# Gathering the rows of two expert pairs in one pass, and the place of the seventh pair's gate weights in the load order

## The chip, the core and the metric

The kernel runs on one core of one Trainium2 chip. The metric is the device time of one launch in microseconds (us). The whole model, a mixture-of-experts block followed by two further layers, is a single program; each engine (TensorE as PE, VectorE as DVE, ScalarE as ACT, GpSimd as POOL) runs its own instruction list and waits on semaphores, and SyncE (SP) issues the weight loads.

## The reference, cut to what matters

The change lies in the mixture of experts of the first block. 256 tokens of width 1024, 16 experts with a hidden width of 512, two experts for each token:

```
def hierarchical_moe(h, w_rg, b_rg, w_re, b_re, w_gate, w_up, w_down):
    ...
    gates = (onehot_g[:, :, None] * w_group[:, None, :]).reshape(-1, N_EXPERTS).astype(t.dtype)
    out = jnp.zeros_like(t)
    for e in range(N_EXPERTS):
        hid = jax.nn.silu(t @ w_gate[e]) * (t @ w_up[e])
        out = out + gates[:, e:e + 1] * (hid @ w_down[e])
    return out.reshape(b, s, d)
```

All of it is float32. What follows, `second_block`, reads `out` after a layer norm and is not touched.

## The kernel before, in words

An expert handles up to 64 tokens ("slots") in a round, and two experts, a **pair**, share the 128 columns of a tile. There are eight pairs, numbered here 0 to 7 (so "pair 6" is the seventh). With these inputs one round is enough, so each pair runs once. Pairs come in twos: an even and an odd one form the body of a loop (`even_and_odd`), whose last turn, pairs 6 and 7, stands behind the loop.

For a pair TensorE does, in this order (`expert_pair`):

- the **gate** product into bank M0 and the **up** product into M1: each is 16 float32 matmuls of 512 columns, two experts side by side, and shows as 32 rows of L1142
- the **scatter** of the pair before, L1106: 8 matmuls that add its output rows to their tokens in S and PT
- four transposes of the hidden rows, L1151, and the turned pick matrix and gate column, L1156 and L1158
- the **gather** of the next pair's rows, L1096: a product of `h_rows` (the tokens) with `pick` (a 0/1 matrix of 256 tokens by 128 slots), in float32, 16 rows into bank MO and 16 into MX
- the **down** product into MO and MX, L1171, which needs the hidden tile that VectorE copies (L2916)

ScalarE copies the gathered rows out of MO and MX (L2031) into `taken_t`; VectorE makes the pick matrices (L2856). Ahead of the loop one gather serves pair 0.

The six weight chunks of a pair (gate, up and down for each expert, 2 MB each) are loaded by SyncE in an order written by hand (`load_gates`, `load_up`, `load_rest`), one queue, strictly one after the other. Gate weights and the first up chunk have two places each, one for even and one for odd pairs. The second up chunk (`up1`) and both down chunks have one place, so they can only be asked for when the pair before has used them up. The waits say so: `gate_done(q)` is M0 filled by pair q, `up_done(q)` is M1 filled, and a down chunk waits for MX to be filled by the pair before.

```
            for p in range(1, PAIRS):
                if p < 4:
                    load_next(p + 1)
                load_rest(p, p, PAIR_CHUNKS[3:4])
                if p == 4:
                    load_next(p + 1)
                load_rest(p, p, PAIR_CHUNKS[4:])
                if 4 < p < PAIRS - 1:
                    load_next(p + 1)
```

Here `load_next(p)` loads the gates and the first up chunk of pair p, `PAIR_CHUNKS[3:4]` is `up1` and `PAIR_CHUNKS[4:]` the two down chunks. For p = 5 the queue is thus: up1 of pair 5, down of pair 5, gates of pair 6, first up chunk of pair 6.

Of the kernel before, what the change touches and what calls it, by code (L numbers as in the profile page):

```python
# [29 lines left out]
F32 = mybir.dt.float32  # L30
# [259 lines left out]
def two_blocks(nc, t, out):  # L290

    with ExitStack() as ctx, nc.allow_non_contiguous_dma(reason="small vectors turned onto partitions"):
# [44 lines left out]
        rounds_f = sb("rounds_f", [P, 5])  # L337
        rounds_i = sb("rounds_i", [1, 4], I32)
# [53 lines left out]
        pick = view(at, TB, P)  # L392
        pick_g = view(at + SEQ, TB, P)
        gate_pair, gate_slot = view(at + 5 * D + 320, TB, 2), view(at + 5 * D + 324, 1, 1)
        taken_t = view(at + D, KD, P)
# [4 lines left out]
        gate_of = view(at + 4 * D + 768, TB, PICKS)  # L400
# [104 lines left out]
        pair_high, pair_low = h_t_r[:, 0:KF, :].rearrange("p k n -> p (k n)"), h_t_r[:, KF:KD, :].rearrange("p k n -> p (k n)")  # L505
# [103 lines left out]
        pick_ready, pick_g_ready = sem("pick_ready"), sem("pick_g_ready")  # L609
        expert_tanhed = sem("expert_tanhed")  # L610
# [41 lines left out]
        def out_count(b, q, last):  # L652

            return b.nth("moe", "taken" if last else "out", q)
# [5 lines left out]
        def _(pe):  # L660
# [427 lines left out]
            def gather(q, name="taken"):  # L1088

                pe.wait_ge(pick_ready, q + 1)  # L1090
                for j, b in enumerate((MO, MX)):
                    claim(b, name, q - 1)
                    for i in range(4):
                        k = 4 * j + i
                        for tb in range(TB):
                            ins = pe.matmul(b.ap[:, i * P:(i + 1) * P], h_rows[:, tb, k * P:(k + 1) * P], pick[:, tb, :],  # L1096
                                            start=tb == 0, stop=tb == TB - 1)
                    ins.then_inc(b.full, 1)

# [14 lines left out]
            gather(0, "taken")  # L1114
# [6 lines left out]
            for b in (MO, MX):  # L1121
                pe.wait_ge(b.free, b.nth("start", "taken"))
            last_even = pe.value_load(rounds_i[0:1, 3:4], min_val=PAIRS - 2, max_val=PAIRS * ROUNDS - 2)
            def expert_pair(q, gate_landed, gate_w, up_landed, up_w, last=False):
# [8 lines left out]
                for b in (MO, MX):  # L1133
                    pe.wait_ge(b.free, q * 2 + 1)
# [3 lines left out]
                for kind, b in enumerate((M0, M1)):  # L1138
                    both_w = [weights_of(e, kind) for e in range(2)]
                    for k in range(KD):  # L1140
                        for lanes, w in zip(halves, both_w):
                            ins = pe.matmul(b.ap[lanes, :], taken_t[:, k, lanes], w[k], start=k == 0, stop=k == KD - 1)  # L1142
                    ins.then_inc(b.full, 1)
                for y in (MO, MX):
                    pe.wait_ge(y.free, q * 2 + 2)
# [14 lines left out]
                if not last:  # L1160
                    gather(q + 1)
# [4 lines left out]
                for half, y in enumerate((MO, MX)):  # L1166
                    if not last:
                        claim(y, "out", q)
# [9 lines left out]
            def even_and_odd(q, last=False):  # L1178
                expert_pair(q, [(expert_landed[e], q * 8 + 16) for e in range(2)], even_w,
# [2192 lines left out]
```

## Time and profile before

| | |
|---|---|
| median of three runs | 1680.19 us (1678.5 to 1682.64) |
| the profiled execution | 1683.05 us |
| its span, first to last instruction | 1681.3 us |
| mean granted TensorE clock | 0.986 |
| PE busy | 1595.3 us, 95% |
| DVE busy | 939.9 us, 56% |
| ACT busy | 653.9 us, 39% |
| the expert pairs | from 359.2 us to 582 us of the span |
| load queue from 340 to 600 us | 91.6% of the 16 DMA engines' time |

Columns of a timeline row: start and length in us, engine, line, operation, output<-inputs, tile shape, count, and in brackets how long the engine sat idle before it and what ended that. A busy PE is one with a matmul in flight; two column halves run side by side, so L1142 at 0.59 us each starts one couple every 0.43 us. The rows of SPq are the issues of loads, not the transfers; the time from issue to landing is a separate line.

### The profile page before, as it was taken

Reading aid. Unit: us, or ns where it says so; the run is one execution under the profiler, and the core shown is the slowest. Engines: PE = TensorE matmul, PEld = TensorE weight load, DVE = VectorE, ACT = ScalarE, POOL = GpSimd, SP = SyncE. Lnnn points to the kernel's source line nnn. Section 1 sums busy time; section 2 is a strip of 40 time slices with the busy share of each in tenths; the row PEclk is TensorE's granted clock in tenths of the full one; section 3 lists DMA queues with packets and bytes.
Section 4 is the critical chain, followed back from the end, with each engine's and each line's share of the span. In section 5 each row is a group of like instructions: output and inputs, shape, how many; then the busy total and the mean of one; then the engine's idle time right before and its main releaser. Section 6 shows DMA issues by size and latency. Waiting matters only on the chain.

```text
span 1681.3 us, 22363 instructions
## 1 busy us (share of the span) xinstructions
PE 1595.3 (95%) x9359; PEld 1239.7 (74%) x9359; DVE 939.9 (56%) x1374; ACT 653.9 (39%) x960; POOL 27.1 (2%) x89
## 2 busy tenths in 40 slices
PE   5999999999999889899999999999999999999998
PEld 1998655454445378687888899988768878889986
DVE  3876666642222265565685666545466567556653
ACT  2543410111111243565644543435365744543441
POOL 1000010100000000000000000000000000000000
PEclk9999999989999989999999999999999999999999
DMA  8555518889989924423354455545424235435651
GB/s 306 189 186 200 202 51 292 328 360 412 413 356 423 390 99 149 126 96 109 145 177 153 143 172 188 200 150 193 153 76 151 101 126 182 169 122 192 201 178 73
DMA packets 153090, 333.33 MB, mean 198 GB/s; under 512 B 17699, under 2 KB 69157, under 8 KB 140709
## 3 DMA queue, kind: packets, MB, share of 16 engines
q1 hardware_dynamic: 147440, 326.94, 53.7%
q10 hardware_dynamic: 5558, 5.06, 0.9%
q8 instruction: 70, 1.15, 0.3%
q14 instruction: 22, 0.18, 0.0%
HBM read 330.94 MB, written 1.05 MB: 197 GB/s over the span
## 4 chain that ended last, share of the span: by engine, by line
PE 80%; DVE 8%; DMA 6%; ACT 4%; issue 1%; POOL 0%; ACTq 0%; POOLq 0%; DVEq 0%; SPq 0%
PE ps_g L737 19%; PE ps_g L718 16%; PE ps_g L1142 6%; PE ps_g L1282 6%; PE ps_s L1538 4%; PE ps_p L1538 3%; PE ps_o L785 3%; PE ps_g L878 3%; DMA arena<-in_w_up_dram 3%; PE ps_p L718 2%; DVE ring_r L2292 2%; DMA ring<-in_w_mod_dram 2%; PE ps_s L718 1%; PE ps_x L691 1%; PE ps_o L1171 1%
## 5 line engine op out<-in xcount | busy, mean ns | idle before, releaser
L2292 DVE TENSOR_TENSOR ring_r<-ring,late_w 128x4096 fp32r<-128x4096 f32 (+1 forms) x50 | 216.9, 4339 | 153.6 <-ACT late_w L1854 153.6
L1854 ACT ACTIVATE late_w<-ring 128x4096 fp32r<-128x4096 f32 (+1 forms) x50 | 178.1, 3563 | 127.9 <-PE ps_p L1538 42.8
L737 PE MATMUL ps_g<-hf_high,ring_r 128*128 128x256 f32 x640 | 178.8, 279 | 0.0
L737 PE MATMUL ps_g<-hf_high,late_w 128*128 128x256 f32 x576 | 162.1, 281 | 0.0
L737 PE MATMUL ps_g<-h_t_r,late_w 128*128 128x256 f32 x576 | 161.2, 280 | 0.0
L737 PEld LDWEIGHTS ps_g<-hf_high,ring_r 128*128 128x128 f32 x640 | 121.9, 190 | 0.0
L737 PEld LDWEIGHTS ps_g<-h_t_r,late_w 128*128 128x128 f32 x576 | 108.6, 189 | 0.0
L737 PEld LDWEIGHTS ps_g<-hf_high,late_w 128*128 128x128 f32 x576 | 108.1, 188 | 0.0
L1878 ACT ACTIVATE arena<-arena,neg_max 128x256 f32<-128x256 f32 (+1 forms) x160 | 71.5, 450 | 40.7 <-DVE neg_max L2347 40.7
L1142 PE MATMUL ps_g<-arena 128*64 128x512 f32 x288 | 85.9, 599 | 0.0
L718 PE MATMUL ps_g<-early_w,first_low 128*128 128x512 f32 (+1 forms) x176 | 68.7, 391 | 3.7 <-ACT arena L1840 1.8
L785 PEld LDWEIGHTS ps_o<-arena 128*128 128x128 f32 x496 | 61.3, 191 | 13.2 <-issue 9.1
L1282 PE MATMUL ps_g<-gate_w,first_low 128*128 128x512 f32 x160 | 67.4, 421 | 1.6 <-ACT arena L2148 1.6
L718 PE MATMUL ps_g<-early_w,h_t_r 128*128 128x512 f32 (+1 forms) x176 | 68.6, 390 | 0.0
L2292 DVE TENSOR_TENSOR ring_r<-ring,early_w 128x4096 fp32r<-128x4096 f32 (+2 forms) x12 | 47.6, 3968 | 36.9 <-ACT early_w L1854 36.9
L718 PE MATMUL ps_g<-ring_r,first_low 128*128 128x512 f32 (+1 forms) x176 | 68.2, 387 | 0.0
L785 PE MATMUL ps_o<-arena 128*128 128x64 f32 (+1 forms) x496 | 61.4, 273 | 6.3 <-ACT arena L1893 3.1
L1282 PE MATMUL ps_g<-gate_w,h_t_r 128*128 128x512 f32 x160 | 63.0, 394 | 0.0
L1282 PE MATMUL ps_g<-ring_r,first_low 128*128 128x512 f32 x160 | 62.9, 393 | 0.0
L2292 DVE TENSOR_TENSOR ring_r<-ring,first_w 128x4096 fp32r<-128x4096 f32 x11 | 48.7, 4425 | 24.7 <-ACT first_w L1854 24.7
L3052 DVE TENSOR_TENSOR ring_r<-ring,gate_w 128x1024 fp32r<-128x1024 f32 x40 | 48.4, 1219 | 24.3 <-ACT gate_w L2123 23.9
L1142 PE MATMUL ps_g<-ring,arena 128*64 128x512 f32 x192 | 55.6, 592 | 2.2 <-issue 2.2
(697 smaller groups left out, 3713.6 us busy)
## 6 DMA issues: line engine op xcount, KB each, us to landing
ring<-in_w_in_dram SPq DMA_DIRECT2D x31, 2048.0 KB, 7.8
ring<-in_w_gate_up_dram SPq DMA_DIRECT2D x44, 1024.0 KB, 7.2
arena<-in_w_down_dram SPq DMA_DIRECT2D x16, 2048.0 KB, 13.5
ring<-in_w_mod_dram SPq DMA_DIRECT2D x10, 2048.0 KB, 10.3
ring<-in_w_down_dram SPq DMA_DIRECT2D x10, 2048.0 KB, 8.0
arena<-in_w_up_dram SPq DMA_DIRECT2D x8, 2048.0 KB, 17.7
ring<-in_w_gate_dram SPq DMA_DIRECT2D x8, 2048.0 KB, 14.5
ring<-in_w_up_dram SPq DMA_DIRECT2D x4, 2048.0 KB, 18.3
```

Source lines behind the costliest of these rows:

```text
L691: ins = pe.transpose(b.ap[0:size, i * SEQ + tb * P:i * SEQ + (tb + 1) * P], piece(tb), ident[:, :])
L718: ins = pe.matmul(b.ap[:, 0:n], x[:, k, tb * P:(tb + 1) * P], a[:, k, lo:lo + n], start=k == 0 and i == 0, stop=k == nk - 1 and i == len(b ...
L737: ins = pe.matmul(b.ap[:, (f % 2) * SEQ:(f % 2 + 1) * SEQ], a[:, k, f * P:(f + 1) * P], x[:, k, :], start=k == 0 and i == 0, stop=k == nk ...
L785: ins = pe.matmul(O.ap[:, i * width:(i + 1) * width], probs_t[:, i, b, :], v(step, i, b), start=b == 0, stop=b == kbs - 1)
L878: ins = pe.matmul(b.ap[:, :], x[:, k, tb * P:(tb + 1) * P], w[:, k, :], start=k == 0, stop=k == KD - 1)
L1142: ins = pe.matmul(b.ap[lanes, :], taken_t[:, k, lanes], w[k], start=k == 0, stop=k == KD - 1)
L1282: ins = pe.matmul(G[tb].ap[:, :], x[:, 2 * q + k, tb * P:(tb + 1) * P], a[:, k, :], start=q == 0 and k == 0 and i == 0, stop=q == KD // 2 ...
L1538: ins = pe.matmul((S, PT)[tb].ap[:, half * HALF:(half + 1) * HALF], a[:, k, tb * P:(tb + 1) * P], x[:, k - 4 * c, half * HALF:(half + 1) * ...
L1854: act.activation(high_of(name, rnd)[:, 0:n], ring[:, slot, 0:n], ACT.Copy).then_inc(high_ready.sem, 1)
L1878: ins = act.activation(s, s, ACT.Exp, bias=neg_max[:, n % 2, i:i + 1], scale=-1.0, accum_out=den[:, n % 4, i:i + 1])
L2292: dve.tensor_tensor(ring_r[:, slot, 0:n], ring[:, slot, 0:n], high_of(name, rnd)[:, 0:n].bitcast(F32), ALU.subtract).then_inc(low_ready.se ...
L3052: dve.tensor_tensor(gate_piece(name, q, ring_r), gate_piece(name, q, ring), gate_high_w[q].bitcast(F32), ALU.subtract).then_inc(gate_low, 1)
```

## The change

Three things are done.

1. The rows of two pairs are gathered at once. `pick` becomes `pick_r`, 256 slots wide. Ahead of the loop there are now two float32 gathers (`first_gather`, pairs 0 and 1). In the loop the gather stands in the odd pair only (`gather_two`) and fetches both pairs of the next turn. It is no longer one float32 product but two in the faster `float32r` format: `h_rows` is split into a high part, made by ScalarE (`routed_high`, four copies), and a low part, made by VectorE (`routed_low`, four subtractions). `taken_t` holds 256 slots, and its second half lies in `h_t`; `pair_low` moves to the arena.
2. Four fillings of MO and MX belong to such a gather in place of two, so the semaphore counts of the down chunks change (`out_count`).
3. For p = 5 the gates of pair 6 are asked for ahead of the down chunks of pair 5, and the first up chunk behind them.

```diff
-            def gather(q, name="taken"):
-
-                pe.wait_ge(pick_ready, q + 1)
+            def first_gather(p):
+
+                pe.wait_ge(pick_ready, p + 1)
                 for j, b in enumerate((MO, MX)):
-                    claim(b, name, q - 1)
+                    claim(b, f"taken{p}")
...
+            def gather_two(q):
+
+                pe.wait_ge(routed_low_ready, len(ROUTED_PIECES))
+                pe.wait_ge(pick_ready, q + 4)
+                for r in range(2):
+                    for j, b in enumerate((MO, MX)):
+                        claim(b, f"taken{r}", q)
+                        for i in range(2):
+                            for tb in range(TB):
+                                for part in range(2):
+                                    ins = pe.matmul(b.ap[:, i * SEQ:(i + 1) * SEQ], routed(part, tb, 4 * r + 2 * j + i), pick_r[:, tb, :],
+                                                    start=tb == 0 and part == 0, stop=tb == TB - 1 and part == 1)
+                        ins.then_inc(b.full, 1)
...
-            gather(0, "taken")
+            for p in range(2):
+                first_gather(p)
...
-                if not last:
-                    gather(q + 1)
+                if odd and not last:
+                    gather_two(two)
...
                 load_rest(p, p, PAIR_CHUNKS[3:4])
                 if p == 4:
                     load_next(p + 1)
+                if p == 5:
+                    load_gates(p + 1, p + 1, gate_done(p - 1))
                 load_rest(p, p, PAIR_CHUNKS[4:])
-                if 4 < p < PAIRS - 1:
+                if p == 5:
+                    load_up(p + 1, up_done(p - 1))
+                elif 5 < p < PAIRS - 1:
                     load_next(p + 1)
...
+            for piece, (tb, lo, n) in zip(routed_high, ROUTED_PIECES):
+                act.activation(piece[:, :], h_rows[:, tb, lo * P:(lo + n) * P], ACT.Copy).then_inc(routed_high_ready, 1)
...
+            def take_two(q):
+
+                for r in range(2):
+                    for j, b in enumerate((MO, MX)):
+                        act.wait_ge(b.full, b.nth("moe", f"taken{r}", q))
+                        act.activation(taken_t[r][:, 2 * j:2 * j + 2, :], b.ap[:, :].rearrange("p (k n) -> p k n", n=SEQ), ACT.Copy).then_inc(b.free, 1)
...
+            for piece, (tb, lo, n) in zip(routed_high, ROUTED_PIECES):
+                cols = slice(lo * P, (lo + n) * P)
+                dve.tensor_tensor(routed_low[:, tb, cols], h_rows[:, tb, cols], piece[:, :].bitcast(F32), ALU.subtract).then_inc(routed_low_ready, 1)
...
+                if not odd and not last:
+                    dve.wait_ge(MX.full, q * 2 + 2)
+                    for p in range(2):
+                        pick_slots(q + 2 + p, pick_r[:, :, p * P:(p + 1) * P], False).then_inc(pick_ready, 1)
```

On TensorE, in an even pair of the loop, between the turned pick matrix and the down product, before:

```order
1003 L1156 MATMUL ps_g<-ident,arena 128x128 x2
1004 L1158 MATMUL ps_g<-arena 128x2 x2
1005 L1090 REGISTER_ALU
1006 L1096 MATMUL ps_o<-arena,h_rows 128x128 x8
1007 L1096 MATMUL ps_x<-arena,h_rows 128x128 x8
1008 L1162 REGISTER_ALU
1009 L1171 MATMUL ps_o<-arena 64x512 x8
1010 L1171 MATMUL ps_x<-arena 64x512 x8
```

and at the same place now:

```order
1010 L1189 MATMUL ps_g<-ident,arena 128x128 x2
1011 L1191 MATMUL ps_g<-arena 128x2 x2
1012 L1195 REGISTER_ALU
1013 L1204 MATMUL ps_o<-arena 64x512 x8
1014 L1204 MATMUL ps_x<-arena 64x512 x8
```

The gather between them is gone; the order counts a float32 matmul once where the trace shows two rows. In the odd pair there stand now 32 matmuls of 256 columns (four fillings like this one, MO, MX, MO, MX):

```order
1044 L1125 MATMUL ps_o<-pick_r,routed_high_65 128x256
1045 L1125 MATMUL ps_o<-pick_r,routed_low 128x256
1046 L1125 MATMUL ps_o<-pick_r,routed_high_66 128x256
1047 L1125 MATMUL ps_o<-pick_r,routed_low 128x256
1048 L1125 MATMUL ps_o<-pick_r,routed_high_65 128x256
1049 L1125 MATMUL ps_o<-pick_r,routed_low 128x256
1050 L1125 MATMUL ps_o<-pick_r,routed_high_67 128x256
1051 L1125 MATMUL ps_o<-pick_r,routed_low 128x256
```

They took the place of the 16 float32 matmuls that stood in each pair.

On SyncE, from up1 of pair 5 on, before (the name in brackets is the semaphore waited for: `expert_g0_full` a gate product, `expert_g1_full` an up product, `expert_x_full` a down product):

```order
56 L1629 DMA arena<-in_w_up_dram 128x2x2048 [waits expert_g1_full]
57 L1629 DMA arena<-in_w_down_dram 128x2x2048 [waits expert_x_full] x2
58 L1629 DMA ring<-in_w_gate_dram 128x2x2048 [waits expert_g0_full]
59 L1629 DMA ring<-in_w_gate_dram 128x2x2048
60 L1629 DMA ring<-in_w_up_dram 128x2x2048 [waits expert_g1_full]
61 L1629 DMA arena<-in_w_up_dram 128x2x2048 [waits expert_g1_full]
62 L1629 DMA arena<-in_w_down_dram 128x2x2048 [waits expert_x_full] x2
```

and now:

```order
56 L1662 DMA arena<-in_w_up_dram 128x2x2048 [waits expert_g1_full]
57 L1662 DMA ring<-in_w_gate_dram 128x2x2048 [waits expert_g0_full]
58 L1662 DMA ring<-in_w_gate_dram 128x2x2048
59 L1662 DMA arena<-in_w_down_dram 128x2x2048 [waits expert_x_full] x2
60 L1662 DMA ring<-in_w_up_dram 128x2x2048 [waits expert_g1_full]
61 L1662 DMA arena<-in_w_up_dram 128x2x2048 [waits expert_g1_full]
62 L1662 DMA arena<-in_w_down_dram 128x2x2048 [waits expert_x_full] x2
```

Two gate loads moved ahead of two down loads; the rest stands as before.

## Rows read from the trace of the kernel before

**Rows 1.** Chain that ended last, 340 to 600 us: start us, us, what.
```profile
359.20 13.95 PE ps_g L1142 x64
...
376.22 1.89 PE ps_o L1096 x16
378.11 1.79 PE ps_x L1096 x16
379.89 3.58 PE ps_o L1171 x16
...
386.91 13.73 PE ps_g L1142 x64
...
428.58 21.69 DMA arena<-in_w_up_dram
450.40 7.09 PE ps_g L1142 x32
...
539.98 22.42 DMA arena<-in_w_up_dram
562.54 8.78 PE ps_g L1142 x32
```

**Rows 2.** Stretches: us, busy of PE PEld DVE ACT POOL, PEclk, DMA share, GB/s.
```profile
380.00:450.00 70.00, 68.74 (x356) 30.30 (x354) 17.91 (x47) 9.91 (x20) 0.00 (x0) 1.00 1.01 416
...
495.00:501.00 6.00, 6.00 (x30) 2.00 (x28) 2.90 (x5) 1.26 (x2) 0.00 (x0) 1.00 0.25 37
...
507.00:562.00 55.00, 53.55 (x286) 25.28 (x282) 13.15 (x34) 7.53 (x16) 0.00 (x0) 1.00 1.01 422
```

**Rows 3.** Timeline of SyncE: the issue of pair 2's gate loads.
```profile
366.32 0.89 SPq L1629 DMA_DIRECT2D ring<-in_w_gate_dram  x2
```

**Rows 4.** Three issues of line L1629, each with its time to landing.
```profile
L1629 SPq DMA_DIRECT2D arena<-in_w_up_dram x1: 368/368/368, 457.5 to 457.5; - x1
DMA to landing us min/median/max: 7.9/7.9/7.9
...
L1629 SPq DMA_DIRECT2D arena<-in_w_down_dram x2: 368/420/471, 498.8 to 499.2; - x2
DMA to landing us min/median/max: 8.1/10.4/12.7
...
L1629 SPq DMA_DIRECT2D arena<-in_w_down_dram x2: 368/419/470, 526.3 to 526.7; - x2
DMA to landing us min/median/max: 10.5/12.7/15.0
```

**Rows 5.** ScalarE's copies around the gather that begins at 460.41, timeline.
```profile
460.95 0.38 ACT L2044 ACTIVATE pick_t<-ps_g 128x256 fp32r<-128x256 f32 x1
462.47 0.60 ACT L2031 ACTIVATE arena<-ps_o 128x512 f32<-128x512 f32 x1 [1.14 <-PE ps_o L1096]
```

**Rows 6.** Float32r matmuls of 256 columns, first and last of twelve, timeline.
```profile
603.56 0.28 PE L1237 MATMUL ps_p<-early_w,first_low 128*128 128x256 f32 x1
...
604.86 0.28 PE L1237 MATMUL ps_p<-early_w,h_t_r 128*128 128x256 f32 x1
```

**Rows 7.** A down product with no gather ahead of it (pair 7), timeline.
```profile
574.79 3.65 PE L1171 MATMUL ps_o<-arena 128*64 128x512 f32 x16 [0.41 <-DVE arena L2916]
```

**Rows 8.** Stretches, columns as in Rows 2: up of pair 3, wait and up of pair 7.
```profile
450.40:457.00 6.60, 6.59 (x32) 2.62 (x32) 0.00 (x0) 0.00 (x0) 0.00 (x0) 1.00 1.01 420
560.50:562.50 2.00, 0.06 (x2) 0.00 (x0) 0.69 (x1) 0.60 (x1) 0.00 (x0) 1.00 1.02 426
562.50:566.00 3.50, 3.46 (x10) 1.31 (x12) 0.00 (x0) 0.00 (x0) 0.00 (x0) 0.60 1.01 419
```

**Rows 9.** Part 5 of the page: a VectorE subtraction of 1024 columns.
```profile
L3052 DVE TENSOR_TENSOR ring_r<-ring,gate_w 128x1024 fp32r<-128x1024 f32 x40 | 48.4, 1219 | 24.3 <-ACT gate_w L2123 23.9
```

**Rows 10.** Timeline: idle time of ScalarE (router) and VectorE (pair 0's first product).
```profile
344.08 0.21 ACT L2009 ACTIVATE rt_s<-rt_s 128x8 f32<-128x8 f32 x1 [4.85 <-DVE rt_s L2827]
...
366.95 0.69 DVE L2911 SCALAR_TENSOR_TENSOR arena<-arena,ps_g 128x512 f32<-128x512 f32 x1 [5.30 <-ACT arena L2038]
```

## What I expect, and why

> **What bounds the kernel now.** I read the chain of waits first. Through the expert pairs it runs on PE but passes twice through a load of `up1`: pair 3's, issued at 428.6 and landed at 450.4, and pair 7's, issued at 540.0 and landed at 562.5 [rows 1]. So ask how busy the load queue is. The table of stretches says 1.01 of its time at 416 GB/s from 380 to 450 us and 422 GB/s from 507 to 562 us; at that rate a 2 MB chunk takes 2.097 MB / 422 GB/s = 4.97 us [rows 2]. A pair has six chunks, 29.8 us. PE's own work on a pair is shorter: the issues at 498.8 and 526.3, each released by the end of a down product, are 27.5 us apart [rows 4]. PE keeps up with the queue only because pairs 0 and 1 lie ready at the start, and it has used up that lead by pair 3, and again by pair 7. The loads set the pace, PE comes close behind, and work taken off PE counts only where a load's issue hangs on PE. Such a place exists: from 495 to 501 us the queue is a quarter busy and moves 37 GB/s [rows 2], because the next in line, the down chunks of pair 5, wait for the down product of pair 4 and are issued at 498.8 [rows 4]. The change puts something into that hole.
>
> **The change part by part.** All times below are of the profiled execution (1683.05 us). I follow five events from before to after; what counts at the end is the shift of pair 7's `up1`, since nothing behind it is changed.
>
> *Start.* The second gather ahead of the loop costs PE 1.89 + 1.79 = 3.7 us [rows 1]. Nothing hides it: pair 0's gate product stands behind it on PE. Pair 0 starts at 362.9 in place of 359.2, and the gate loads of pair 2, which wait for that product and are issued at 366.3 [rows 3], at 370.0. Of the four new copies on ScalarE (2048 columns; at 0.60 us for 512 [rows 5] 2.4 us) all lie in its idle 4.85 us, VectorE's subtractions (two times 1.2 us [rows 9]) and one more pick matrix in its idle 5.30 us, lengthened by 3.7 [rows 10]: nothing. Without that cover they would cost 2.4 us each.
>
> *PE's work on a pair.* A gather in the loop was 3.7 us for one pair. Now 32 matmuls of 256 columns fetch two. Twelve such start within 603.56 to 604.86, eleven distances in 1.30 us, 0.118 each [rows 6], so 3.8 us. To that come waits on ScalarE, which must empty MO before its second filling: a copy starts 0.2 us after the bank is full and takes 0.60 [rows 5], 0.8 against the 0.94 us that PE spends on MX meanwhile, so nearly hidden. I take 4.1 us; the bounds are 3.8, and 6.2 if all three handovers of 0.8 us lay open. In an even pair the gather goes, and with it the cover of VectorE's copy of the hidden tile. Pair 7, which never had a gather, shows the price: an idle 0.41 us ahead of its down product [rows 7]; I take 0.5. Even pair: 27.5 - 3.7 + 0.5 = 24.3 us. Odd pair: 27.5 - 3.7 + 4.1 = 27.9 us. In a row of two pairs PE saves 2.8 us, beside loads of 59.6 us.
>
> *Up to pair 3's `up1`.* The queue is full from pair 2's gates on [rows 2], so all of it shifts by 3.7: landed at 450.4 + 3.7 = 454.1. PE gets there at 362.9 + 24.3 + 27.9 = 415.1, has pair 2's gates done at 422.0, and waits for that pair's `up1` (six chunks ahead of pair 3's: 454.1 - 29.8 = 424.3) 2.3 us; then 424.3 + 6.9 + 3.0 (scatter and transposes) + 0.5 + 7.0 = 441.7, gates done at 448.6. It now waits 5.5 us for pair 3's `up1`, and the savings so far are gone.
>
> *The clock.* After 2.0 us of idle time at 560.5 the granted clock was 0.60 in the next 3.5 us, mostly its lower level of 1.2 GHz, and pair 7's up product took 8.78 us, where pair 3's, at clock 1.00, took 7.09 [rows 1, 8]: 1.7 us. Pair 3 waits longer than that now, so I charge the same there: its up product ends at 454.1 + 7.1 + 1.7 = 462.9, and pair 4's `up1` goes out then and not at 457.5: 5.4 us late [rows 4]. The bounds are 0 and two such losses, 3.4.
>
> The Trainium skill ("TensorE: Matmul & The Clock Gate", section "HAM oscillation") says that matmul bursts between DMA waits come back throttled each time; here pair 7 bears it out (clock 0.60) and pair 3, with a wait of 1.7 us, does not (1.00). Taken to the letter it adds losses at other waits, which is the third rival below. The same page, section "Back-to-back issue gap", gives N / 2.4 + 2.5 ns, which is 109 ns for 256 columns; by it the double gather would be an estimated 3.5 us instead of 3.8 and the sum below 0.3 us less. The row says 118 ns.
>
> *Pair 4.* Before, PE set the pace from 457.5 to 498.8, while the queue ran ahead of it. Now: `up1` lands at 462.9 + 7.9 = 470.8 [rows 4], then two gate chunks, one up chunk and two down chunks of pairs 5 and 4: + 5 x 4.97 = 495.7. PE is at pair 4's down product at 462.9 + 3.0 + 4.1 + 7.0 + 13.8 + 3.5 = 494.3 and waits 1.4 us. Down product done at 502.7.
>
> *The reordered loads.* Pair 5's `up1` 500.7, then pair 6's gates without a hole 510.6, pair 5's down chunks (issued at 502.8) 520.6, the up chunk 525.5, pair 6's `up1` 530.5. The price of the reorder is that pair 5's down chunks land two chunks later than in the old order (502.8 + 12.7 = 515.5 [rows 4]); PE needs them at 502.7 + 13.8 + 3.0 + 4.1 = 523.6, 3.0 us after they are there, so nothing. That is the cover, and it is 3.0 us thick.
>
> *What is late next.* Pair 6's down chunks wait for pair 5's down product, which ends at 530.6. They are issued then into a queue that ran dry at 530.5, a new hole of some 3 us: landed at 530.7 + 8.1 and 4.97 later, 543.8. Before, they were issued at 526.3 behind other loads, and the second landed at 526.7 + 15.0 = 541.7 [rows 4]. From there to pair 7's `up1` both orders load the same chunks, none of which PE releases late (it is through pair 6's up product at 544.4).
>
> *Sum.* 543.8 - 541.7 = +2.1 us. In parts: + 3.7 start, + 1.7 clock, + 0.4 double gather in pair 5, - 6.7 hole at 495 closed, + 3.0 new hole. Pair 7 waits for its `up1` as before, some 2 us, with the same clock loss. 1683.05 + 2.1 = 1685.2 for the profiled execution. It lies 2.9 us above the median of the runs, so the shift is put on the median: 1680.2 + 2.1 = 1682.3 us. A measurement of this kernel tells 0.3%, 5.0 us, from no change; this is within it.
>
> **The rivals.** *The clock does not fall at pair 3* (it did not after 1.7 us of idle time [rows 8]): the same sum without 1.7, 1680.6. Same verdict.
>
> *PE sets the pace after all.* This would need the queue to deliver faster than 4.97 us for a chunk. Then the change is worth what it takes off PE: seven gathers in the loop, 25.9 us, become three of 4.1 and four idle bits of 0.5, 14.3; less 3.7 at the start: - 7.9, 1672.3 us. Against it stand the share of 1.01 and two loads on the chain [rows 1, 2]. A milder form is that the new hole before pair 6's down chunks doesn't open, because PE gets through pair 5 some 3 us sooner: - 0.9.
>
> *Slower: the throttled clock spreads.* Waits that PE had twice it now has four times: pair 2 (2.3 us), pair 3 (5.5), pair 4's down chunks (1.4), pair 7. At pair 4 a loss of 1.7 us falls on the path, since pair 5's down product releases the next loads; a second 1.7 at pair 3 does too, for a wait of 5.5 us is longer than any in the rows here. 2.1 + 1.7 + 1.7 = + 5.5, 1685.7 us. It decides from an idle time of somewhere between 1.7 and 2.0 us on [rows 1, 8]. The rule of the Trainium skill on the clock (page and section above), taken to the letter, ends here.
>
> *The change doesn't do what it says*, for instance if the gates of pair 6 were not free to load at 490.8: they are, pair 4's gate product ended 7 us before. No chance of its own.
>
> **How the numbers follow.** Forecast with one clock loss 0.55, no clock loss 0.22, spread clock 0.13, faster PE-bound or mild 0.10. Predicted 1682.3, that of the likeliest. The range takes in both clock cases with the bounds of the gather (3.8 to 6.2 on pair 5: - 0.3 to + 2.1) and of the clock, and some of the mild faster case: 1677.5 to 1686. Slower than 1685.2 is most of the spread case, 0.09; faster than 1675.2 needs most of the PE-bound one, 0.06; within 0.3% is left with 0.85.
>
> **What would show it.** In the profile of the changed kernel: pair 0's first L1175 row about 363 us; the gather of 32 rows about 4 us in odd pairs; PE's wait for pair 3's `up1` some 5.5 us with a low granted clock behind it; a DMA share near 1.0 from 495 to 501 us, and a dip of 3 us about 530; pair 7's up product starting near 564 to 565. I am wrong if the queue is not full between pair 2's gates and pair 3's `up1`, if the hole at 530 is missing, or if pair 0 does not start later.

## The result, and the profile after

The changed kernel takes 1685.28 us in the median of 22 runs (1681.32 to 1690.38), the kernel before, timed beside it, 1683.14 us (22 runs, 1678.5 to 1685.47). The ratio is 1.0018, with a 95% interval of 1.001 to 1.0026: 1.7 to 4.4 us slower. Timed again later (a_fifth below): 1.002, 1.0008 to 1.0032. The shift of the medians is the +2.1 us of the prediction, and 1685.28 lies in its range; its verdict, that this cannot be told from no change, is wrong. The slowdown is small but it is there. The predicted 1682.3 us was counted from 1680.19, the median of three runs; the kernel before, timed beside the change, lies 3.0 us above that, and this is the distance from 1682.3 to 1685.28.

The profiled execution took 1683.26 us (span 1681.5) at a mean clock of 0.986; before it was 1683.05 (1681.3), also 0.986. These two executions alone would say +0.2 us. So one execution of each does not show where the time went.

The chain that ended last, 340 to 600 us (start us, us, what), answers to [rows 1]:

```profile
357.91 1.79 PE ps_o L1111 x16
359.69 1.80 PE ps_x L1111 x16
...
363.63 13.97 PE ps_g L1175 x64
378.03 16.79 DMA arena<-in_w_up_dram
...
402.92 21.70 DMA arena<-in_w_up_dram
...
432.20 22.23 DMA arena<-in_w_up_dram
454.57 8.90 PE ps_g L1175 x32
...
466.52 1.07 PE ps_o L1125 x8
467.59 0.93 PE ps_x L1125 x8
468.52 0.96 PE ps_o L1125 x8
469.48 0.93 PE ps_x L1125 x8
...
477.91 18.42 DMA arena<-in_w_down_dram
496.58 3.65 PE ps_o L1204 x16
...
545.13 19.81 DMA arena<-in_w_up_dram
565.08 7.09 PE ps_g L1175 x32
```

The second float32 gather stands ahead of pair 0, which starts at 363.63. The chain now passes through loads five times, not twice: up1 of pairs 1, 2, 3 and 7 and the down chunks of pair 4. Pair 1's up1 lands at 394.82 and its up product starts at 394.96, so it costs next to nothing. Pair 3's up product took 8.90 us where it took 7.09. The double gather in an odd pair is four fillings, 466.52 to 470.41 (469.48 + 0.93): 3.9 us.

Stretches of the same execution (us, busy of PE PEld DVE ACT POOL, PEclk, DMA share, GB/s), to be held against [rows 2] and [rows 8]:

```profile
380.00:450.00 70.00, 66.57 (x331) 27.96 (x329) 19.02 (x52) 10.10 (x22) 0.00 (x0) 1.00 1.01 422
451.00:454.00 3.00, 0.00 (x0) 0.00 (x0) 0.00 (x0) 0.00 (x0) 0.00 (x0) 0.57 1.01 421
454.50:462.00 7.50, 7.43 (x27) 2.62 (x28) 0.00 (x0) 0.00 (x0) 0.00 (x0) 0.75 1.00 415
495.00:501.00 6.00, 4.42 (x22) 1.89 (x24) 1.15 (x5) 0.00 (x1) 0.00 (x0) 1.00 1.02 426
525.00:532.00 7.00, 7.00 (x34) 2.30 (x32) 1.97 (x3) 0.63 (x1) 0.00 (x0) 1.00 0.75 312
```

The queue is full from 380 to 450 us; the hole at 495 us is closed (share 0.25 before, 1.02 now); a new one stands at 525 to 532 us, where a quarter of 7 us is missing. In pair 3's wait the clock falls (0.57) and is at 0.75 behind it.

SyncE's issue of pair 2's gates [rows 3] and of pair 4's up1 [rows 4]:

```profile
370.75 0.89 SPq L1662 DMA_DIRECT2D ring<-in_w_gate_dram  x2
...
463.50 0.37 SPq L1662 DMA_DIRECT2D arena<-in_w_up_dram  x1
```

### The profile page after: what moved, and what is told of

It reads as the page before. It is cut to its first block, busy times and chain, and to the rows that moved or that the text cites. A ratio compares the mean times of both kernels' runs of the same rounds, so it can differ in the third digit from the quotient of the medians.

```text
span 1681.5 us, 22176 instructions
## 1 busy us (share of the span) xinstructions
PE 1584.5 (94%) x9263; PEld 1229.9 (73%) x9263; DVE 943.3 (56%) x1377; ACT 655.8 (39%) x964; POOL 27.1 (2%) x89
## 4 chain that ended last, share of the span: by engine, by line
PE 77%; DMA 9%; DVE 8%; ACT 4%; issue 1%; SPq 0%; POOL 0%; ACTq 0%; POOLq 0%; DVEq 0%
PE ps_g L752 19%; PE ps_g L733 16%; PE ps_g L1315 6%; DMA arena<-in_w_up_dram 5%; PE ps_g L1175 4%; PE ps_s L1571 4%; PE ps_p L1571 3%; PE ps_o L800 3%; PE ps_g L893 3%; PE ps_p L733 2%; DVE ring_r L2338 2%; DMA ring<-in_w_mod_dram 2%; PE ps_s L733 1%; PE ps_x L706 1%; PE ps_g L1538 1%
## 5 line engine op out<-in xcount | busy, mean ns | idle before, releaser
L800 PEld LDWEIGHTS ps_o<-arena 128*128 128x128 f32 x496 | 61.3, 191 | 13.2 <-issue 9.1
L3106 DVE TENSOR_TENSOR ring_r<-ring,gate_w 128x1024 fp32r<-128x1024 f32 x40 | 48.5, 1220 | 24.3 <-ACT gate_w L2169 23.9
L2282 ACT ACTIVATE arena<-arena 128x512 f32<-128x512 f32 x22 | 13.9, 632 | 105.7 <-DVE arena L3332 105.7
L752 PE MATMUL ps_g<-first_high,first_w 128*128 128x256 f32 x192 | 54.8, 286 | 0.1
```

The lines of the kernel that those rows point to most:

```text
L752: ins = pe.matmul(b.ap[:, (f % 2) * SEQ:(f % 2 + 1) * SEQ], a[:, k, f * P:(f + 1) * P], x[:, k, :], start=k == 0 and i == 0, stop=k == nk ...
L800: ins = pe.matmul(O.ap[:, i * width:(i + 1) * width], probs_t[:, i, b, :], v(step, i, b), start=b == 0, stop=b == kbs - 1)
L3106: dve.tensor_tensor(gate_piece(name, q, ring_r), gate_piece(name, q, ring), gate_high_w[q].bitcast(F32), ALU.subtract).then_inc(gate_low, 1)
```

## One execution is not enough: ten profiles of the two kernels

Both kernels were profiled again, unchanged.

b_again, b_third and b_fourth are the kernel before:

> The kernel before once more, word for word: another profiled execution. If the size of the clock losses is set by the code, the low stretches lie where they lay (one in the experts, at pair 7's up product, and the experts' stretch from the router's start is 243.5 us within 0.5 us). If they differ between executions, the stretch moves by 1.7 us or a multiple of it, and the start of the router too.

> The kernel before word for word, a third profiled execution: experts' stretch 222.7 to 223.1 us as in the two so far, if its single loss at pair 7 falls every time; 221.2 us if it can fail to come. Start 20.7 us, or 19.2 as in e1_loads_only.

> The kernel before word for word, a fourth profiled execution. So far the experts' stretch was 222.5 to 223.1 us, the start 20.8, 20.7 and 19.2 (with a low clock in pair 0), the rest 1099.4, 1100.7 and 1099.2 us with 1, 2 and 1 low stretches. Expected in these bounds. If low stretches behind the experts come with the changed kernel only, none or one here; if they come by chance, up to three as in e1_loads_only.

a_again, a_third, a_fourth, a_fifth and a_sixth are the changed kernel:

> The changed kernel once more, word for word: another profiled execution. Loads are expected where they were (wait of pair 3 5.8 us, up product 8.9, double gather 3.9, down of pair 6 landed 180.2 us after pair 0's first gate matmul). Pair 7's up product is 7.1 us again if its clock is set by the code, and 8.8 if it differs between executions.

> The changed kernel word for word, a third profiled execution. It tells how often the clock falls behind pair 4's wait: once in two so far. Low clock behind pair 3's wait of 5.8 us expected every time, experts' stretch (pair 0's first gate matmul to the end of pair 7's down product) 219.2 us without a second loss and 220.8 with it.

> The changed kernel word for word, a fourth profiled execution. As for a_third: experts' stretch 219.2 us or 220.8 us. Its start (router's first matmul to pair 0's first gate matmul) 24.4 us or 22.5 us.

> The changed kernel word for word, timed once more beside the kernel before, with a fifth profile. Over the runs so far its mean granted clock was 0.9848 (25 runs) where the kernel before had 0.9885 (64 runs), and 0.001 of clock goes with some 0.8 us. If the clock carries the slowdown, this shows again: clock lower by 0.003 or more and ratio 1.0015 to 1.003. If the difference was chance among the runs: clocks equal and ratio 1.000 to 1.001.

> The changed kernel word for word, a sixth profiled execution. In the four so far the experts' stretch was 219.2 to 220.8 us, the start 24.4, 22.5, 22.7 (with a low clock in pair 0) and 21.1 (the same), and the rest of the program 1098.6 to 1103.0 us by the number of low stretches in it (0, 2, 3, 3). Expected in these bounds; a rest above 1103.5 or below 1098.5 would speak against the count of low stretches as what sets it.

Measured, in us. "Start" is from the router's first matmul (`route_w`) to pair 0's first gate matmul, "experts" from there to the end of pair 7's down product, "rest" from there to the end of the span. A low stretch is one in which the granted clock was 0.5, its lower level of 1.2 GHz. Those at about 590 us and at the very end are in every execution and not counted. Pair 0's gate in brackets: its product ran in such a stretch without a wait for a load. What lies ahead of the router's first matmul is not in the table: 338.4 to 340.6 us in the four executions of before (mean 339.6), 338.7 to 341.6 us in the six of after (340.4).

| execution | start | experts | rest | low stretches in the rest, from 600 us on | lost behind a wait |
|---|---|---|---|---|---|
| before | 20.8 | 222.7 | 1099.4 | 1 | pair 7 |
| b_again | 20.7 | 223.1 | 1100.7 | 2 | pair 7 |
| b_third | 19.2 | 222.5 | 1099.2 | 1 | none (pair 0's gate) |
| b_fourth | 20.7 | 220.6 | 1099.4 | 1 | none |
| after | 24.4 | 219.2 | 1098.6 | 0 | pair 3 |
| a_again | 22.5 | 220.8 | 1100.9 | 2 | pair 3, pair 4's down |
| a_third | 22.7 | 220.0 | 1103.0 | 3 | pair 3 (pair 0's gate) |
| a_fourth | 21.1 | 220.1 | 1102.9 | 3 | pair 3 (pair 0's gate) |
| a_fifth | 21.1 | 219.8 | 1100.0 | 1 | pair 3 (pair 0's gate) |
| a_sixth | 22.5 | 220.5 | 1102.2 | 3 | pair 3, pair 4's down |

b_again alone looked as if the code set the losses: its start and experts took 243.8 us (expected 243.5 within 0.5) and its loss stood at pair 7 again. b_third and b_fourth refute that. b_fourth's experts (220.6 us) lie below the bounds expected for it, as a loss at neither place had not been seen before. a_third and a_fourth (220.0 and 220.1) hit neither of the two values expected, 219.2 and 220.8. a_fifth and a_sixth came as expected. In a_again pair 6's down chunks landed 181.8 us behind pair 0's first gate matmul and not the expected 180.2: its second loss was passed on to the next loads.

Three things follow.

**The clock losses differ between executions of one program.** b_third has no loss at pair 7, a_again has a second one at pair 4's down product. The same rows in three executions of the kernel before (pair 7's first up matmul, with the idle time ahead of it in brackets), then in the changed kernel's first two profiles (pair 4's down product). Of before:

```profile
562.54 0.61 PE L1142 MATMUL ps_g<-x_rows,arena 128*64 128x512 f32 x1 [1.99 <-DMA arena<-in_w_up_dram]
```

of b_again, and of b_third:

```profile
564.98 1.01 PE L1142 MATMUL ps_g<-x_rows,arena 128*64 128x512 f32 x1 [2.30 <-DMA arena<-in_w_up_dram]
```

```profile
564.45 0.61 PE L1142 MATMUL ps_g<-x_rows,arena 128*64 128x512 f32 x1 [1.72 <-DMA arena<-in_w_up_dram]
```

of after, and of a_again:

```profile
496.58 3.65 PE L1204 MATMUL ps_o<-arena 128*64 128x512 f32 x16 [2.36 <-DMA arena<-in_w_down_dram]
...
565.08 0.61 PE L1175 MATMUL ps_g<-x_rows,arena 128*64 128x512 f32 x1 [2.76 <-DMA arena<-in_w_up_dram]
```

```profile
496.85 5.35 PE L1204 MATMUL ps_o<-arena 128*64 128x512 f32 x16 [2.01 <-DMA arena<-in_w_down_dram]
...
567.25 0.61 PE L1175 MATMUL ps_g<-x_rows,arena 128*64 128x512 f32 x1 [2.94 <-DMA arena<-in_w_up_dram]
```

16 rows of the down product take 3.65 us behind an idle time of 2.36 us and 5.35 us behind one of 2.01. Pair 7 waits 2.6 to 2.9 us in the changed kernel and loses nothing in any of its six profiles; behind 1.99 and 2.30 us the kernel before lost 1.7 us. Two variants below did lose the clock at pair 7, e7_down_sooner behind 2.78 us (its up product took 8.78 us) and e2_gather_only behind 2.93 us (8.47 us). Only pair 3's wait of 5.6 us lost every time, 1.4 to 2.3 us. So the length of an idle time between 1.7 and 2.9 us does not say whether the clock falls.

**The rest is the same work.** It takes 1098.6 us without a low stretch, 1099.2 to 1100.0 with one, 1100.7 to 1100.9 with two, 1102.2 to 1103.0 with three: some 1.4 us each. With one stretch it is 1099.2 to 1099.4 us before and 1100.0 in a_fifth, where the stretch at about 590 us is longer too (13.6 us, not 10.2); with two, 1100.7 and 1100.9. They fall at five places (about 708, 827, 1201, 1247 and 1364 us), a different choice in each execution.

**All the runs together.** Each run also gives its mean granted clock. Mean values over the runs of this study; the last column takes out the clock at 0.82 us for 0.001, which is the common slope of a straight line through the 88 runs of before and the 38 of after. e5, e6, a_again and b_again ran on a second chip, where the kernel before took 1682.4 us in the mean (1681.3 to 1682.3 in the other series):

| kernel | runs | mean us | against before | mean clock | at like clock |
|---|---|---|---|---|---|
| before | 88 | 1682.2 | | 0.9884 | |
| after | 38 | 1685.8 | +3.6 | 0.9849 | +0.7 |
| e1_loads_only | 11 | 1680.4 | -1.9 | 0.9879 | -2.3 |
| e2_gather_only | 7 | 1687.1 | +4.9 | 0.9856 | +2.5 |
| e3_split_start | 11 | 1683.0 | +0.7 | 0.9848 | -2.2 |
| e4_ballast | 9 | 1687.8 | +5.6 | 0.9852 | +3.0 |
| e5_best | 10 | 1678.2 | -4.0 | 0.9855 | -6.4 |
| e6_best_old_gather | 11 | 1678.6 | -3.6 | 0.9883 | -3.7 |
| e7_down_sooner | 11 | 1683.4 | +1.2 | 0.9857 | -1.0 |
| e8_up1_sooner | 12 | 1684.6 | +2.4 | 0.9859 | +0.3 |

At like clock the two kernels differ by 0.7 us (standard error 0.4). The line puts the other 2.9 us of the 3.6 down to a clock that is lower by 0.0035. Every kernel with the double gather has such a clock, 0.9848 to 0.9859; the three with the old gather have 0.9879 to 0.9884. a_fifth asked in fresh runs whether the lower clock and the longer time were chance, and both came again: clock 0.9851 against 0.9883, ratio 1.002. But the last column is a regression, no experiment, and it does not show that the clock is the cause. The mean clock also counts low time in which TensorE only waits: in the profile of after, 3.2 of the 6.8 us at pair 3 lie ahead of its up product (the low stretch begins at 451.4, the product at 454.57). By the line 0.001 of mean clock is worth 0.82 us; one low stretch in the rest takes as much off the mean and costs some 1.4 us, one in a wait costs nothing. In the ten profiles the mean clock differs by 0.001 only (0.9871 and 0.9861), so they do not show where the 0.0035 of all the runs comes from.

## The experiments

**One part alone.** e1_loads_only is the kernel before with the new load order (below), e2_gather_only the changed kernel without these lines:

```diff
+                if p == 5:
+                    load_gates(p + 1, p + 1, gate_done(p - 1))
                 load_rest(p, p, PAIR_CHUNKS[4:])
-                if 4 < p < PAIRS - 1:
+                if p == 5:
+                    load_up(p + 1, up_done(p - 1))
+                elif 5 < p < PAIRS - 1:
```

> The kernel before with the load order of the change alone (gates of pair 6 ahead of the down chunks of pair 5), the gathers as they were. My theory (the loads set the pace, each hole in the queue counts): the hole at 495 us closes, pair 6's down chunks land at 539.0 in place of 541.7, pair 7's up1 at 559.7 in place of 562.4, before PE asks for it at 560.5. Pair 7's wait of 2.0 us and the clock loss of 1.7 us behind it go: 3.7 us faster than the kernel before, ratio 0.9978, clock 1.00 from 355 to 585 us. Rival A (the reorder is what makes the change slower, since pair 5's down chunks land later): slower by 2 us or more. Rival B (it does nothing): 1.000.

> The change without its new load order: both gathers ahead of the loop and the double gathers, the loads in the old order. My theory: 3.7 us late from the start, 1.8 us of clock at pair 3, and the hole ahead of pair 5's down chunks is there again (issued at 503.7, landed at 511.8 and 516.8), so pair 7's up1 lands about 567.3: 4.9 us slower than the kernel before, ratio 1.0029, and some 2.5 us slower than the change. Rival (PE sets the pace, the gathers pay): 7.9 us faster, 0.995.

e1: 1679.78 us, ratio 0.9988 (0.9976 to 0.9999). e2: 1686.54 us, ratio 1.0035 (1.0019 to 1.005). So the load order gains 2.0 us (0.2 to 4.0), the gathers with their start lose 5.9 us (3.2 to 8.4), and the two sum to +3.9 us, which the whole change has within the intervals (+3.0). The signs are the expected ones, and both intervals hold the ratio expected and exclude the rivals; e1's median gain is smaller than the 3.7 us of the arithmetic. In its profile pair 7 waits no more, but pair 0's gate product ran at the low clock, and three low stretches lie in the rest (1101.9 us), with the old gather.

**The start.** e3_split_start is the changed kernel with the gather ahead of the loop made like that in it (float32r, two parts), and VectorE's subtractions moved ahead of the pick matrices (`fill_two` is the body of `gather_two`):

```diff
-            for p in range(2):
-                first_gather(p)
+            first_gather()
...
+                pe.wait_ge(routed_low_ready, len(ROUTED_PIECES))
+                pe.wait_ge(pick_ready, 2)
+                fill_two(lambda b, name: claim(b, name))
```

> The change with the rows of pairs 0 and 1 also gathered by the float32r product of high and low parts (32 rows of 0.118 us in place of 64 of 0.112), VectorE's subtractions moved ahead, into its idle time before the places come. My theory: pair 0 starts some 3.0 us earlier than in the change, all loads from pair 2's gates on with it, and the end too: 3.0 us faster than the change, about 1 us faster than the kernel before (0.9995). Rival (the start is hidden, since weights wait for nothing that early, or the time is given back at pair 3): same as the change, 1.0015.

1683.06 us, ratio 1.0009 (0.9999 to 1.002). The expected 0.9995 is outside the interval, the rival's 1.0015 inside; the ratio is 0.0009 below the changed kernel's, which is 1.5 us in place of 3 and less than the two intervals tell apart. Its start took 22.9 us in one profile, which says little, as that of the changed kernel lies anywhere from 21.1 to 24.4. Its rows say why the start gained less than the 3 us, a row of VectorE's timeline first and then the chain:

```profile
352.25 1.39 DVE L2902 TENSOR_SCALAR pick_r<-arena 128x64 fp32r<-128x64 f32 x8 [0.16 <-DVE arena L2894]
...
351.65 2.09 issue
353.74 2.05 PE ps_o L1111 x8
355.79 1.71 PE ps_x L1111 x8
357.50 1.71 PE ps_o L1111 x8
359.20 1.34 PE ps_x L1111 x8
```

TensorE waits 2.09 us, until both pick matrices are made (352.25 + 1.39), and runs the gather at the low clock (granted 0.5 from 353.1 to 359.9 us): 6.8 us for the work that takes 3.9 in the loop.

**The clock at pair 3.** e4_ballast is the changed kernel with its loop written out and 11 matmuls more ahead of pair 3's up product, whose result is thrown away; they fill the wait but for 0.55 us:

```diff
-            with pe.Fori(0, last_even, 2) as q:
-                even_and_odd(q)
+            for q in range(0, PAIRS - 2, 2):
...
+                    if kind == 1 and isinstance(q, int) and q in (3,):
+                        for _ in range(11):
+                            pe.matmul(M1.ap[:, 0:SEQ], ident[:, :], tri[:, :], start=True, stop=True)
```

> The change with 11 matmuls of no use (float32, 256 columns, some 4.7 us in all) in pair 3 between its gate and up product, where PE waits 5.1 us for up1, the loop over pairs written out on TensorE so that only pair 3 has them. My theory: the clock stays at its upper level, pair 3's up product takes 7.1 us and not 8.9, and the 1.8 us reach the end: 1.8 us faster than the change, ratio to the kernel before about 1.0005. Rival (the clock loss is absorbed by the loads behind it, as PE is not the bound): same as the change, 1.0015 to 1.0018. A third outcome, that the clock loss only moves to the next wait (pair 4's down chunks), would show as 1.00 at pair 3 and a low clock at 497 us.

1687.98 us, ratio 1.0038 (1.0024 to 1.0051): not faster, and above both what was expected (1.0005) and the rival (1.0015 to 1.0018). The third outcome named is the one that came. Its stretches around pair 3's up product and pair 4's down product:

```profile
454.50:461.00 6.50, 6.30 (x30) 2.65 (x32) 0.00 (x0) 0.00 (x0) 0.00 (x0) 1.00 1.01 418
492.00:496.20 4.20, 1.00 (x9) 0.69 (x9) 1.78 (x9) 0.71 (x3) 0.00 (x0) 1.00 1.02 423
496.20:500.00 3.80, 3.80 (x12) 1.35 (x10) 0.00 (x0) 0.00 (x0) 0.00 (x0) 0.55 1.01 420
```

The clock holds at pair 3 (1.00), TensorE then waits longer at pair 4's down chunks (3.2 us where it was 2.0 to 2.4), and the loss is there (0.55). What is saved ahead of a load that sets the pace turns into a longer wait at the next. Why this kernel is slower still than the changed one is open: its loop is written out as well, and its one profile has four low stretches in the rest (1104.7 us).

**Moving one wait.** e8_up1_sooner puts pair 3's up1 ahead of pair 4's first up chunk, e7_down_sooner puts pair 4's down chunks ahead of pair 5's first up chunk; nothing else differs from the changed kernel. In the order of one step p (g: gates of pair p + 1, u: its first up chunk, 1: up1 of p, d: down of p):

```
              p = 1     2     3     4     5     6
before        gu1d  gu1d  gu1d  1gud  1dgu  1dgu
after         gu1d  gu1d  gu1d  1gud  1gdu  1dgu
e7            gu1d  gu1d  gu1d  1gdu  1gdu  1dgu
e8            gu1d  gu1d  g1du  1gud  1gdu  1dgu
```

> The changed kernel with one step of the load order moved: for p = 3 up1 of pair 3 ahead of the first up chunk of pair 4. Its wait (5.8 us in the changed kernel) should shrink to about 0.8 us and the low clock behind it go. Theory (the queue sets the pace up to pair 4's down chunks): the time saved at pair 3 is waited for at pair 4's down product, now 5 to 6 us, since its chunks still land at about 496; pair 6's down chunks land where they did, and the ratio stays at 1.0018 (1.001 to 1.0025). Rival (the wait and the clock loss at pair 3 are what costs): pair 4's down product starts 3 us or more earlier and the ratio is 0.999 or below.

> The changed kernel with one step of the load order moved: for p = 4 the down chunks of pair 4 ahead of the first up chunk of pair 5. They land 4.97 us sooner, so TensorE finds them there (before: a wait of 2.3 us, in one profile with a low clock behind it). Theory (the wait at pair 4's down product and the clock loss it sometimes brings are the part of the slowdown that the prediction sized too small): pair 4's down product starts at once at about 493 to 494 us, the product is 6.9 us in every execution, and pair 6's loads, which follow pair 5's down product, come 1.7 to 2.3 us sooner: ratio to before 1.0018 - 0.001 to - 0.0024 = 0.9995 to 1.0008. Rival (pair 5's and 6's loads are set by the queue alone): 1.0018, as the changed kernel.

e8: 1685.17 us, ratio 1.0015 (1.0004 to 1.0026), as the theory of the queue has it. Its chain:

```profile
450.21 7.09 PE ps_g L1175 x32
...
471.75 23.07 DMA arena<-in_w_down_dram
494.82 0.24 issue
495.06 5.75 PE ps_o L1204 x16
```

and a stretch of it, columns as before:

```profile
488.00:495.00 7.00, 0.05 (x1) 0.00 (x0) 1.31 (x9) 0.71 (x3) 0.00 (x0) 0.82 1.03 427
```

Pair 3's up product is back at 7.09 us and starts 3.6 us sooner by pair 0's clock; pair 4's down chunks land at 494.8, only 0.7 us sooner by the same clock, TensorE stands idle for 7 us (busy 0.05 of the 7.00 from 488 to 495 us) and loses the clock there. The wait moved and grew, and the time stayed. So neither the wait of pair 3 nor the clock loss behind it is what sets pair 4: the queue does. e7: 1683.39 us, ratio 1.0012 (1.0003 to 1.0021). Pair 4's down product waits no more, but pair 6's down chunks land only 0.7 us sooner counted from pair 0, where 1.7 to 2.3 were expected; the interval holds both what the theory gives at its upper end and the rival, so the time decides nothing.

**An order without holes.** e5_best is e3_split_start, e6_best_old_gather the kernel before, with only the load order changed (a and b: one of the two gate chunks):

```
              p = 1     2     3     4     5     6
e6            gu1d  gu1d  1gud  1gdu  1gdu  1dgu
e5            gu1d  gu1d  g1du  1gdu  1gdu  1adbu
```

> The kernel before, its gathers untouched, with the load order altered: up1 of pair 3 ahead of pair 4's gates, gates of the next pair ahead of the down chunks for pairs 4 and 5. Theory: the wait of pair 3 (1.7 us in before) and that of pair 7 with its clock loss (2.0 and 1.7) go, PE sets the pace all through: -4.8 to -5.8 us, ratio 0.997; up product of pair 7 about 7.1 us with no wait. Rival: the order was never the limit, and e1_loads_only's gain of 0.0012 is all there is: 0.999.

> The changed kernel with the gather of pairs 0 and 1 in the faster format too (as in e3_split_start), and with the load order altered at four places so that no issue hangs on a late product: up1 of pair 3 ahead of the up0 of pair 4, gates of the next pair ahead of the down chunks for pairs 4, 5 and 6 (in pair 6 one gate chunk ahead and one behind), so that the hole before pair 6's down chunks has something in it. Theory (loads and PE's lead set the end, the clock takes back a part): holes and waits of pairs 3 and 7 go, PE sets the pace, and what the gathers save on it counts in full: three gathers of 3.9 and four idle bits of 0.5 in place of seven of 3.7, -12.2 us, +2.1 for the later start as e3 showed it, +1.7 for a clock loss at pair 0, and a wait or two left: -6 to -7 us, ratio 0.996. Rival (the clock loss moves along with any lead that is saved, as in e4_ballast): the gain is halved, ratio 0.998. Against the theory altogether: 1.000 or above.

e6: 1678.76 us, ratio 0.9977 (0.9968 to 0.9986). e5: 1679.07 us, ratio 0.9974 (0.9962 to 0.9986). Both beat both kernels; e6 does it with the order alone. The 0.997 expected for e6 is in its interval; the 0.996 expected for e5 is not, the halved gain of its rival (0.998) is. The stretches of e6:

```profile
380.00:450.00 70.00, 70.00 (x367) 31.50 (x367) 17.33 (x46) 9.53 (x20) 0.00 (x0) 1.00 1.00 409
495.00:501.00 6.00, 6.00 (x30) 1.99 (x28) 3.12 (x8) 1.26 (x2) 0.00 (x0) 1.00 1.01 421
```

TensorE is busy for 70.00 of 70 us, the queue is full too, and no row of the expert pairs waits for a load. There the two are in balance. In e5, with less work on TensorE, the chain goes through loads again, and TensorE stands idle 0.6 to 2.0 us ahead of five products:

```profile
400.73 21.82 DMA arena<-in_w_up_dram
422.60 7.11 PE ps_g L1171 x32
429.72 17.69 DMA arena<-in_w_up_dram
...
469.06 18.09 DMA arena<-in_w_down_dram
487.40 5.22 PE ps_o L1200 x16
...
496.87 20.11 DMA arena<-in_w_down_dram
```

Its experts take 214.4 us against e6's 218.6, but its start is 2.7 us longer, and behind the experts its profile has three low stretches where e6's has one (1102.7 against 1099.0 us). By the line through the runs it would lead by 2.7 us at like clock; timed, the two are the same.

## Why the prediction was wrong, point by point

**What bounds the kernel: right.** From pair 2's gates to pair 4's down chunks the queue sets the pace of the changed kernel, and e8 shows it: a wait taken away in one place came back at the next. TensorE is as close behind as the prediction has it; with the loads in better order (e6) it is busy for 70.00 of 70 us.

**Start: right in size.** The second gather cost 1.79 + 1.80 us, and pair 0 began 24.4 us behind the router's first matmul where it was 20.8: +3.6 against a forecast of +3.7. What was not foreseen is that the clock can give some back ahead of it: the first gather began 13.2 us behind the router's first matmul in all four profiles of before, 11.4 to 11.6 us in four of six of after, where fewer of the router's matmuls met the low clock (granted clock from 338 to 351 us: 0.74 in before, 0.87 in a_fifth).

**TensorE's work on a pair: right.** Double gather 3.9 us, forecast 4.1 (bounds 3.8 to 6.2). The formula behind the prediction's 109 ns is one that the Trainium skill ("TensorE: Matmul & The Clock Gate", section "Back-to-back issue gap") gives for a matmul by itself, and not for a stream of weight loads and matmuls; here the 32 took 0.122 us each. Even pair 24.2 us (363.63 to 387.8), forecast 24.3.

**Waits up to pair 4: right, one mis-sized.** Pair 2 waits 1.8 us (2.3), pair 3 5.6 (5.5), pair 4's down 2.4 (1.4). Pair 4's up1 was issued at 463.50 (462.9) and landed 8.05 us later (7.9). Pair 4's down chunks landed at 496.3 (495.7).

**The reordered loads and the new hole: right.** Pair 5's up1 landed at 501.3 (500.7), pair 6's gates at 511.5 (510.6), pair 6's up1 at 531.4 (530.5), pair 6's down chunks at 543.8 (543.8), behind a hole in which the share was 0.75 for 7 us. Pair 5's down chunks, the delayed ones, were not waited for.

**The sum of the loads and gathers: right as far as can be seen.** In the profile pair 7's up1 landed at 564.9 us where it had landed at 562.4: +2.5 against +2.1. Without its clock term the sum was +0.4 us; the line through the runs says +0.7 at like clock.

**The clock: the term that was mis-sized.** The prediction charged 1.7 us once, at pair 3 ("I charge the same there"), took pair 7's loss as the same on both sides, and put the program behind the experts at nothing ("since nothing behind it is changed"). The loss at pair 3 came in six of six profiles and was 1.4 to 2.3 us; a second at pair 4's down product came in two of six. That at pair 7 came in two of four before and in none of six after: in the first profiles the up product behind it took 8.78 us and then 7.09, and 1.7 of the 2.5 us were given back there. In the start and the experts together the profiles show no net difference (before 242.6 us in the mean of four, after 242.5 of six, by the table). The +2.2 us by which their spans differ in the mean lie outside: 0.8 ahead of the router and 1.6 in the rest, where more low stretches fell (2.0 against 1.25 in the mean). The work there is unchanged; the clock it gets is not. By the line through all the runs the clock carries 2.9 us (0.0035 at 0.82 us for 0.001) where the prediction had 1.7; that is a correlation, and no experiment changed the clock alone.

**The bound of 0.3%: the step that failed.** The chance of 0.85 for "within" took 5 us as the least that can be told. With 22 runs of each the interval was 1.6 thousandths wide, and 1.000 lay outside it. The likeliest case, +2.1 us, lies inside the measured 1.7 to 4.4 us and should have been called a slowdown that enough runs can show. That the medians differ by just the +2.1 is in part luck: by all the runs it is +3.6, and in the profiles the difference of the spans lies outside the stretch that the prediction added up.

**The rivals.** The spread clock (0.13, 1685.7 us) is near the 1685.28 only because the kernel before was slower too; its shift of +5.5 us lies outside 1.7 to 4.4. Its loss at pair 3 came in every profile, its second loss, at pair 4, in two of six. Its deciding point, "an idle time of somewhere between 1.7 and 2.0 us on", is refuted: 2.36 us idle without a loss, 2.94 us without a loss, 2.01 us with one. The Trainium skill ("TensorE: Matmul & The Clock Gate", section "HAM oscillation") describes a kernel whose bursts come back throttled behind every DMA wait, and gives these as some 3 to 5 us. For pair 3's 5.6 us the traces agree, six of six; carried over to shorter waits, as this rival did, the rule fails: in 8 of the 10 profiles pair 7 waits 1.7 to 2.9 us and goes on at full clock. No clock fall at pair 3 (1680.6) and TensorE as the bound (1672.3) did not come.

**What stays open.** Why the kernels with the double gather run at a clock lower by 0.003 in the mean. e5_best has it with less waiting than the changed kernel, so pair 3's wait is not the whole of it; e1 and e6 do not have it. That TensorE, with less to do beside the same loads, stands idle in more places would fit, and was not shown. Nor does any run show what part of it belongs behind the experts and what is chance. Over all the profiles of this study the rest took 1101.3 us in the mean of the 12 with the double gather (1098.6 to 1104.7) and 1100.0 in that of the 6 with the old one (1099.0 to 1101.9): the ranges overlap, and so few cannot tell them apart.

## What to carry to other kernels

Where loads set the pace, as here, work taken off the engine turns into waits, and behind a wait the clock can be lost; put the order of the loads right first (e6_best_old_gather: 3.9 us for no change in work), then see if the engine binds. And read a small difference from many runs with their clocks beside them, not from one profile of each: here one pair of profiles said +0.2 us, 126 runs said +3.6.

## What the runs showed of the hardware

- Executions of one program lose the clock at different places. The rest of this kernel, the same instructions each time, took 1098.6 to 1103.0 us by the number of low stretches in it (0 to 3), and over 126 runs of the two kernels a run's time went with its mean granted clock, 0.82 us for 0.001.
- Idle times of 1.7 to 2.9 us were followed by full clock or by a low one (0.60 behind 1.99 us, 0.63 behind 2.04 us in a_sixth) without order by their length.
- In the stretches shown in which its share was 1.00 or more, the load queue moved 409 to 427 GB/s on this one core; in the holes it moved 37 (before, 495 to 501 us) and 312 GB/s (after, 525 to 532 us).
